# Where the first weight splits and small copies of a linear-attention decoder kernel stand on ScalarE and VectorE

## What is computed

```python
def block(x, mem_k, mem_v, conv_buf, s_gla, s_gdn, chunked, g_mix, w_in, ...):
    h = rmsnorm(x, g_mix)
    proj = jnp.einsum('btd,de->bte', h, w_in)
    gq, gk, gv, gr, glr, cqkv, dz, da, db = jnp.split(proj, _split_points(IN_SIZES), axis=-1)
    ...
    xc = jnp.concatenate([conv_buf.astype(cqkv.dtype), cqkv], axis=1)
    conv = jax.nn.silu(sum(xc[:, j:j + T] * gdn_conv_w[j] for j in range(CONV_W)))
    new_buf = xc[:, T:]
    cq, ck, cv = jnp.split(conv, [GDN_KW, 2 * GDN_KW], axis=-1)
    ...
    x = x + jnp.einsum('bte,ed->btd', o, w_out)
    x = x + cross_attention(rmsnorm(x, g_xattn), mem_k, mem_v, xa_w_q, xa_w_o)
    h = rmsnorm(x, g_ffn)
    ff = jax.nn.silu(jnp.einsum('btd,df->btf', h, ffn_w_gate)) * jnp.einsum('btd,df->btf', h, ffn_w_up)
    x = x + jnp.einsum('btf,fd->btd', ff, ffn_w_down)
```

## Time and profile before

| | us |
|---|---|
| median of 3 runs | 1855.31 |
| lowest and highest run | 1855.22 and 1855.92 |
| the profiled execution | 1854.26 |
| its span, first to last instruction | 1851.9 |
| TensorE busy in it | 1814.0 (98%) |
| VectorE busy | 1150.0 (62%) |
| ScalarE busy | 796.2 (43%) |
| GpSimd busy | 183.2 (10%) |

### The profile page before, as it was taken

The page is one execution under the profiler, slowest core; times in us unless marked ns, Lnnn a source line. Parts: engine busy times, 40 slices in busy tenths (PEclk is TensorE's granted clock), DMA queues, the critical chain, the costliest instruction groups (busy, mean ns, idle before and its releaser), DMA issues.

```text
span 1851.9 us, 34219 instructions
## 1 busy us (share of the span) xinstructions
PE 1814.0 (98%) x13818; PEld 1723.1 (93%) x13818; DVE 1150.0 (62%) x1573; ACT 796.2 (43%) x842; POOL 183.2 (10%) x185
## 2 busy tenths in 40 slices
PE   8999999999999999999999999999999999999997
PEld 6999999988999999888749999999999999999997
DVE  6888447746766577555676656666544566665443
ACT  6454545343363533443642344443333444443344
POOL 5000000002106300000005500000000000000231
PEclk9999999999999999999999999999999999999999
DMA  8555554472045667797784688886456899984553
GB/s 266 162 166 174 180 167 155 137 241 76 17 154 177 216 211 247 276 311 250 251 283 128 190 239 249 250 249 193 129 183 193 239 249 248 249 225 134 170 187 110
DMA packets 415128, 367.19 MB, mean 198 GB/s; under 512 B 11519, under 2 KB 374014, under 8 KB 414486
## 3 DMA queue, kind: packets, MB, share of 16 engines
q1 hardware_dynamic: 387368, 340.76, 60.0%
q10 hardware_dynamic: 27678, 25.26, 4.2%
HBM read 347.84 MB, written 18.35 MB: 198 GB/s over the span
## 4 chain that ended last, share of the span: by engine, by line
PE 89%; DVE 5%; ACT 2%; issue 1%; POOL 1%; DMA 1%; DVEq 0%; ACTq 0%; POOLq 0%
PE ps L467 65%; PE ps L543 9%; PE ps L524 4%; DVE w_lo L446 2%; PE ps L961 1%; PE ps L510 1%; PE ps L1245 1%; ACT w_hi L439 1%; PE ps L1260 1%; PE ps L1163 1%; PE ps L1084 1%; PE ps L1402 1%; DMA gst<-in_state_gla_dram 1%; PE ps L1448 1%; PE ps L1440 1%
## 5 line engine op out<-in xcount | busy, mean ns | idle before, releaser
L439 ACT ACTIVATE w_hi<-raw 128x2048 fp32r<-128x2048 f32 (+1 forms) x285 | 512.3, 1797 | 857.6 <-PE ps L467 709.9
L446 DVE TENSOR_TENSOR w_lo<-raw,w_hi 128x2048 fp32r<-128x2048 f32 (+1 forms) x285 | 620.1, 2176 | 261.3 <-ACT w_hi L439 258.1
L467 PE MATMUL ps<-act_hi,w_lo 128*128 128x264 f32 x2560 | 732.8, 286 | 6.2 <-DVE w_lo L446 4.1
L467 PE MATMUL ps<-act_lo,w_hi 128*128 128x264 f32 x2560 | 725.4, 283 | 0.0
L467 PE MATMUL ps<-act_hi,w_hi 128*128 128x264 f32 x2560 | 724.9, 283 | 0.0
L467 PEld LDWEIGHTS ps<-act_hi,w_lo 128*128 128x128 f32 x2560 | 482.2, 188 | 10.6 <-issue 3.9
L467 PEld LDWEIGHTS ps<-act_lo,w_hi 128*128 128x128 f32 x2560 | 482.5, 188 | 0.4
L467 PEld LDWEIGHTS ps<-act_hi,w_hi 128*128 128x128 f32 x2560 | 480.0, 187 | 0.0
L467 PE MATMUL ps<-ff_hi,w_lo 128*128 128x264 f32 x704 | 201.1, 286 | 0.0
L467 PE MATMUL ps<-ff_hi,w_hi 128*128 128x264 f32 x704 | 200.1, 284 | 0.0
L467 PE MATMUL ps<-ff_lo,w_hi 128*128 128x264 f32 x704 | 199.4, 283 | 0.0
(11 more groups left out here) (444 smaller groups left out, 2172.9 us busy)
## 6 DMA issues: line engine op xcount, KB each, us to landing
raw<-in_w_in_dram SPq DMA_DIRECT2D x56, 1024.0 KB, 7.5
raw<-in_ffn_w_gate_dram SPq DMA_DIRECT2D x44, 1024.0 KB, 5.7
raw<-in_ffn_w_up_dram SPq DMA_DIRECT2D x44, 1024.0 KB, 5.7
raw<-in_ffn_w_down_dram SPq DMA_DIRECT2D x32, 768.0 KB, 4.8
raw<-in_ffn_w_down_dram SPq DMA_DIRECT2D x32, 640.0 KB, 6.1
raw<-in_w_out_dram SPq DMA_DIRECT2D x16, 1024.0 KB, 6.3
raw<-in_xa_w_q_dram SPq DMA_DIRECT2D x16, 1024.0 KB, 6.7
raw<-in_xa_w_k_dram SPq DMA_DIRECT2D x16, 1024.0 KB, 6.3
```

The source lines that it names most:

```text
L439: act.activation(w_part(ph, w_hi[b]), raw_part(ph, r, half), ACT.Copy)\
L446: dve.tensor_tensor(w_part(ph, w_lo[b]), raw_part(ph, r, half), w_part(ph, w_hi[b]), ALU.subtract)\
L467: mm = pe.matmul(ps[:, acc(ph, u), 0:ph.cols], w[b][:, k, :], v[:, kk + k, 0:ph.cols], start=first and k == 0 and m == 0, stop=last and k ...
```

## The change

It has three parts. On ScalarE, the high half of the first gdn unit moves from behind the 16 tiles to ahead of tile 13. On VectorE, the copies of `cols` and `convw` move from behind the first gdn low half to ahead of tile 13, with a count of `cols_turned` and of `cols_ready` of their own; the copies of `cst` stay where they were and raise a third count, which TensorE now awaits ahead of the second gdn unit, not of the first (there it awaits the second). And the first four gdn units on VectorE are written out ahead of the loop, with the low half of unit n+2 ahead of the take of unit n instead of behind it; the loop starts at its second pass and keeps its order. The line numbers of the new kernel are higher by 2 to 14.

```diff
--- before.py
+++ after.py
@@ -1003,19 +1003,21 @@
                     pe.wait_ge(cols_ready, 1)
                     pe.wait_ge(rows_landed, 16 * 8)
                     turn(ps[:, 1, P:P + 87 - KT], grows[:, :])
-                    turn(ps[:, 1, 2 * P:2 * P + CW * CT], cwrows[:, :])
+                    turn(ps[:, 1, 2 * P:2 * P + CW * CT], cwrows[:, :]).then_inc(cols_turned, 1)
                     pe.wait_ge(crows_landed, 16)
                 if k >= 10:
                     for t in range(4 * (k - 10), 4 * (k - 9)):
                         mm = turn_conv(t)
-            mm.then_inc(cols_turned, 1)
+                    if k == KT - 1:
+                        mm.then_inc(cols_turned, 1)
             for k in range(KT):
                 strip_products(k)
             pe.wait_ge(x_ready, KT)
             sum_squares(1, TT)
-            pe.wait_ge(cols_ready, 2)
             ph = PH["gdn"]
             for u in range(4):
+                if u < 2:
+                    pe.wait_ge(cols_ready, 2 + u)
                 products(pe, ph, 0, u, act_hi, act_lo)
             with pe.Fori(1, ph.loops) as i:
                 for u in range(4):
@@ -1727,13 +1729,14 @@
             for k in range(KT):
                 if k == 10:
                     split(PH["strip"], 0, 0)
+                if k == 13:
+                    split(PH["gdn"], 0, 0)
                 act.wait_ge(x_taken, k + 1)
                 act.activation(x[:, k, :], ps[:, W4 + k % 4, 0:TT], ACT.Copy).then_inc(x_ready, 1)
                 act.wait_ge(x_ready, k + 1)
                 if k >= 4:
                     act.wait_ge(ssq_ready, k - 3)
                 act.activation(xsq[:, k % 4, :], x[:, k, :], ACT.Square).then_inc(sq_ready, 1)
-            split(PH["gdn"], 0, 0)
             act.wait_ge(consts_ready, 1)
             split(PH["gdn"], 0, 1)
             rms(1, TT, D)
@@ -2110,10 +2113,10 @@
             def split(ph, i, u):
                 split_lo(dve, ph, i, u)
 
-            def run(name, take, nxt):
+            def run(name, take, nxt, first=0):
 
                 ph = PH[name]
-                with dve.Fori(0, ph.loops - 1) as i:
+                with dve.Fori(first, ph.loops - 1) as i:
                     for u in range(4):
                         take(ph, i, u)
                         split(ph, i, u + 2) if u < 2 else split(ph, i + 1, u - 2)
@@ -2151,23 +2154,34 @@
             for k in range(KT):
                 if k == 11:
                     split(PH["strip"], 0, 0)
+                if k == 13:
+                    dve.wait_ge(cols_turned, 2)
+                    dve.tensor_copy(cols[:, KT:87], ps[:, 1, P:P + 87 - KT])
+                    dve.tensor_copy(convw[:, :], ps[:, 1, 2 * P:2 * P + CW * CT]).then_inc(cols_ready, 1)
                 dve.wait_ge(x_turned, k + 1)
                 halves_of(k, ps[:, W4 + k % 4, 0:TT], GAIN_MIX, act_hi, act_lo, x_taken)
             split(PH["gdn"], 0, 0)
-            dve.wait_ge(cols_turned, 2)
-            dve.tensor_copy(cols[:, KT:87], ps[:, 1, P:P + 87 - KT])
-            dve.tensor_copy(convw[:, :], ps[:, 1, 2 * P:2 * P + CW * CT])
+            dve.wait_ge(cols_turned, 3)
             for m in range(2):
                 ins = dve.tensor_copy(cst[:, 12 * m:12 * m + 12, :].rearrange("p t (j b) -> p t b j", j=3),
                                       ps[:, 2 + m, 0:288].rearrange("p (t b j) -> p t b j", t=12, j=3))
             ins.then_inc(cols_ready, 1)
-            dve.wait_ge(cols_ready, 2)
+            dve.wait_ge(cols_ready, 3)
             split(PH["gdn"], 0, 1)
             dve.wait_ge(rstd_ready, 1)
             dve.wait_ge(consts_ready, 2)
             tile_wait(dve, PH["strip"], 0, 0)
             dve.tensor_tensor(strip[:, :], ps[:, 0, 0:TT], rstd[:, :], ALU.mult).then_inc(acc_free, 1)
-            run("gdn", gdn, "gla")
+            ph = PH["gdn"]
+            split(ph, 0, 2)
+            gdn(ph, 0, 0)
+            split(ph, 0, 3)
+            gdn(ph, 0, 1)
+            split(ph, 1, 0)
+            gdn(ph, 0, 2)
+            split(ph, 1, 1)
+            gdn(ph, 0, 3)
+            run("gdn", gdn, "gla", first=1)
             def b3(v, n):
                 return v.unsqueeze(1).broadcast_to([P, n, P])
```

## The result

| | before | after |
|---|---|---|
| median of 5 runs, us | 1855.31 | 1863.31 |
| lowest and highest run | 1853.5 and 1856.9 | 1860.37 and 1864.81 |
| the profiled execution | 1854.26 | 1862.9 |
| its span | 1851.9 | 1861.1 |

The changed kernel is slower: ratio 1.0043, 95% interval 1.0029 to 1.0056, or 8.0 us by the medians. The forecast was 1862.0, with a range of 1860.6 to 1864.8.

The account below looks back on a forecast made before the run. TensorE, busy for 98% of the span, was taken to bound the kernel. With 0.23 us gained and 6.97 lost, net +6.7 on the median of 1855.31 gave 1862.0 us, range 1860.6 to 1864.8.

Parts of the forecast that it names:

- Opening: Before the gdn stage: early high half and small copies start the first unit 0.7 us earlier, of which 0.23 is kept.
- hi(u0): ScalarE's high half of the first gdn unit's weights: could start after the square of tile 12 (24.39), not at 27.51.
- u0: First of the 24 gdn units on TensorE: starts right behind the sum of squares, near 32.5 instead of 33.20.
- hi(u2): ScalarE's high half of the third gdn unit's weights: can start at 39.08 instead of 39.31.
- The chain: First gdn units: high half, low half, take, tail and Silu form one closed loop through VectorE and ScalarE, 7.56 against 5.80.
- first turn: From the third gdn unit's high half to the fourth's, with a table load before the Silu: 8.97 us.
- further turns: From the fourth gdn unit's high half to the fifth's and on to the sixth's, without a table load: 7.56 us each.
- u6: Seventh gdn unit on TensorE, yardstick for the end's delay: starts at 76.56 instead of 69.82, 6.7 us late.
- lo(u6): VectorE's low half of the seventh gdn unit's weights, first from the unchanged loop: 74.12, behind the fifth unit's 3.84 us take.
- The clock: Rival: TensorE's clock falls in new waits, such as 3.2 us before the seventh gdn unit; 1863.4 to 1866.8 us, chance 0.08.
- Absorbed later: Rival: part of the delay vanishes where TensorE waits 1.9 us for a DMA at L1163; 1860.1 us, chance 0.03.
- Faster: Rival: low halves early throughout the gdn stage remove TensorE's waits, gaining 5.7 us; 1849.6 us, chance 0.02.

Follow-up runs that it names:

- the kernel with one low half early: Changed kernel with only the third gdn unit's low half ahead of the first take, later takes first: 1857.72 us, repeated 1857.37 us.
- the high half ahead of the Silu: Changed kernel with ScalarE making its first high halves one step earlier, ahead of tail and Silu, VectorE unchanged: 1855.60 us.
- the kernel with the order alone: Kernel before with only VectorE's first four gdn units written out, low half ahead of take, opening unchanged: 1863.91 us.
- the filled waits: Changed kernel with 16, 10, 10 and 20 unused matmuls on TensorE ahead of the fourth to seventh gdn units: 1862.80 us.
- the kernel with the opening alone: Changed kernel with VectorE's gdn stage back in its loop of before, early high half and moved small copies kept: 1855.38 us.

## Why the prediction held, step by step

- **Opening.** Right: hi(u0) at 24.72, the last square at 28.39 (forecast end near 29.1, measured 28.8), u0 without a wait. u0 itself started at 33.58, not 32.5, because in this execution the strip's matmuls went over to 0.12 us only at 30.64, where they had at 27.79 before. This differs from execution to execution with the same opening: in the two traces of the kernel with one low half early it comes at 28.23 and 29.50, in that of the high half ahead of the Silu at 28.07. The later start moves the whole stage: hi(u2) starts at 40.37, not 39.08, 1.29 us later than forecast.
- **The chain.** Right in mechanism and nearly in size: a first turn of 9.07 against 8.97, further turns of 7.70 and 7.69 against 7.56. Two terms were small: from high to low half, when VectorE waits for it, are 2.0 us and not 1.93 (49.44 to 51.44), and the tail follows the take's start by 3.05 (53.65 to 56.70) and not 2.97.
- **u6.** Forecast 76.56, measured 78.33: 1.29 by hi(u2), 0.37 by the three turns, 0.11 by the rest from hi(u5) on. So the chain cost what was worked out, within 0.5 us. I had lo(u6) come right behind take(u4), with hi(u6) ready at the same moment; measured, hi(u6) is the later of the two, by 0.28.
- **The clock.** I gave it 0.08 as a rival to my forecast, and called 2.4 us the longest wait inside the trace. That holds only behind the opening: the same list has one of 4.0, at L961, which ends at 3.95. The fall is no rival but an addition, and in the profiled execution it came: the waits before u3 and u6 both end with a fallen clock, shown below. At u3 the wait that I had forecast before u4 (1.7) swallows it: u4 starts at 61.48 with none; at u6 nothing does, and the first matmuls of the unit come 0.22 apart (78.64 to 81.72: 14 steps), 1.4 us in all, as the rival had it. That they agree so well is luck, since the size differs from execution to execution: in the kernel with the order alone u6 took 8.5 us (77.36 to 85.90) behind the same wait, against 5.9 before.
- **Absorbed later.** The rival was right in kind for a small part: the wait for the state of the GLA heads (L1163 before) is 1.3 us instead of 1.9. In the end the spans differ by 9.2: 8.5 at u6 and 1.5 for the slow start of u6, less some 0.3 in the stage and 0.6 at that wait.
- **Faster.** The rival put the old waits of TensorE up to u20 and the lead at u6 at 5.7 us, 1849.6. The size was right: without those waits the kernel takes 1849.34. But it is VectorE's fixed addresses in all 24 units that remove them, and I named only an early low half.
- **The sum.** Forecast +6.7; the chain without the clock, as the filled waits show it, +7.0; the medians +8.0. So the term that was too small is mainly not in the chain: it is the clock, which I had left out of the likeliest case. It makes about 1 us of the 8, by the difference of the two, which sets one execution against a median. The one run of the changed kernel with a mean clock of 0.998 took 1860.37, 6.1 over the profiled execution of before at the same clock (6.7 by the spans, 1858.6 and 1851.9), and the others took 1862.9 to 1864.8 at 0.994 to 0.996.

## What to carry to other kernels

An order that serves one engine is judged on all the engines that hand work around: write down what each instruction waits for, follow it until it comes back to the same engine, add up the turn, and compare it with the pace of the engine that must not wait. Here moving one operation ahead of another on VectorE joined two parallel branches into one loop of 7.70 us against 5.80, and putting ScalarE's high half ahead of its Silu opened it again without touching VectorE. And of a new wait on TensorE, price the clock too: on top of waits of 2.5 to 3.1 us it cost another 1.4 to 2.6 here, in some executions. Where an engine is just too slow for the pace, look at the form of its code first: the same take took 2.97 us with fixed addresses and 3.4 to 3.8 in the loop, and that was worth 6 us.

## What the runs showed of the hardware

**TensorE's clock also falls in waits that did not touch it in the trace before.** The changed kernel, in windows of 1 us (length, busy us of PE, PEld, DVE, ACT, POOL, granted clock, DMA share, GB/s):

```profile
54.00:55.00 1.00, 1.00 (x7) 1.00 (x8) 0.93 (x4) 0.00 (x0) 0.00 (x0) 0.78 0.02 7
55.00:56.00 1.00, 1.00 (x6) 1.00 (x6) 0.93 (x5) 0.00 (x0) 0.00 (x0) 0.50 0.80 146
...
58.00:59.00 1.00, 1.00 (x10) 1.00 (x9) 0.00 (x0) 1.00 (x1) 0.00 (x0) 1.00 1.09 348
...
79.00:80.00 1.00, 1.00 (x7) 1.00 (x6) 0.86 (x4) 0.57 (x1) 0.00 (x0) 0.50 0.00 0
```

After waits of 2.55 and 3.07 us the granted clock goes from 2.4 to 1.2 GHz (0.50), and comes back within the unit. And in the kernel with the opening alone it fell behind the wait of 2.4 us at L1262 (L1260 before), whose stretch had 1.00 in the trace before:

```profile
456.00:457.00 1.00, 1.00 (x7) 1.00 (x6) 0.29 (x1) 0.00 (x0) 0.00 (x0) 0.50 1.10 356
```

The same wait, of the same length, thus costs the clock in one execution and not in another, and this also holds within one kernel: the wait of 2.54 us before u3, in the two traces of the kernel with one low half early, left it at 1.00 the first time and brought it to 0.50 the second, for 1.5 us. The 3.7 us between those two executions are, nearly all, this fall, one like it near 507, and a later start of the stage, where the strip's matmuls go from 0.22 to 0.12 apart at 28.23 and at 29.50. (That the clock makes this last difference isn't shown: the granted clock reads 1.00 on both sides of it.) It fits the spread of the other kernels: of the 22 runs of the kernel before in the second session, the five with a mean clock of 0.998 took 1853.4 to 1854.7, the four with 0.994 or 0.995 took 1856.9 to 1859.1. With 16 matmuls into an unused bank in the wait, two of eleven runs had a mean clock of 0.995, where seven of twelve had it without them.

**A table load had no drain beside it here either**: in the changed kernel the tail ends at 47.81, the load runs from 47.82 to 49.10, and the Silu starts at 49.11.
